# A two-layer trunk with 16 experts: one fixed tile per expert with its products in a new order, and the extra tiles in a loop of their own

## The chip, the core and the metric

The kernel runs on one core of one Trainium2 chip. The metric is the device time of one launch in microseconds (us). The engines are TensorE (PE in the profile, its weight loads PEld), VectorE (DVE), ScalarE (ACT), GpSimd (POOL) and SyncE (SP, which here only issues loads).

## The reference

Two layers (DEPTH = 2) work on 640 tokens of 1024 channels: 512 latent tokens and 128 context tokens. Each layer has an attention branch and a convolution branch, which are merged and projected, and then a mixture of experts. The change touches only the last:

```python
scores = softmax(t @ w_router)                  # 16 experts
# the best of 4 groups, then the best two experts in it; wsel: their scores, made to sum to 1
combine = sum(one_hot(eidx, 16) * wsel[..., None], axis=1)
hg = einsum('td,edf->tef', t, w_gate)           # 1024 -> 256
hu = einsum('td,edf->tef', t, w_up)
h = silu(hg) * hu * combine[..., None]
y = einsum('tef,efd->td', h, w_down)            # 256 -> 1024
```

All data are float32. Each token goes to 2 of 16 experts, so there are 1280 (token, expert) pairs in a layer, 80 an expert on average.

## The kernel before

Float32 products are made from two halves of each operand: a high half, which ScalarE writes as the engine's rounded format (hi, for experts `hi_expert`, L883), and a low half, raw minus high (lo, on POOL L1849 or VectorE L1222). A product takes three matmuls: high by high, high by low, low by high (`MM3`). Weights come in units of 1 MB through four raw buffers of 8 KB per partition: a load of unit n waits until unit n - 4 has its low half (`raw_free`). All engines have their programs written out by hand, and semaphores join them; the order in each engine's program is the order of its work.

An expert has three units. Before the change units 0 and 1 are the two halves of the 1024 input rows, with gate and up side by side (four pieces of 512 KB, in runs of 1 KB), unit 2 is down (runs of 4 KB).

**The routing** (VectorE L1564 to L1702) turns the router's logits into slots. TensorE's product with a triangle of ones gives each pair's place among its expert's pairs, a second product the counts (L688, L689; `place`). The pairs are sorted into tiles of 128 rows: an expert has ceil(count/128) tiles, at least one, and the tiles of all experts stand one behind the other. POOL writes ten columns of rows (token, target row, weight) into the table `tab_d` in memory (L1908), reads it back as `tab` (L1780), makes the low half of down of expert 0 (L1849), and starts to gather.

**The experts.** Every engine walks over the experts and, inside, over a loop with bounds that are read from `start_i` at run time (`value_load`). For a tile TensorE does, in this order: gate/up (24 matmuls, L718), the transposes of h (L724), the transposes of the next tile's gathered rows (8, L702), down (12 matmuls, L734). ScalarE does Silu (`sg`, L1168), the high halves of h (L1170) and of the gathered rows (L1134), drains down's result from PSUM to `ye` (L1141), and at an expert's start makes the high halves of the next expert's three units. VectorE does `hx` (L1731), the low halves of h (`ht_lo`, L1734) and of the gathered rows (`xt_lo`, L1713), and the low halves of the next expert's units. POOL gathers rows of `u2_d` by the table (L1931) and sends rows of `ye` to `y_d` (L1951). A table row that belongs to no pair gathers token 0; its send is skipped by the bounds check.

Of the next stage the experts' end releases this: ScalarE waits for the last send and reloads all results (`y_in`, L1178), VectorE adds them to `ha_in` (loaded by ScalarE's queue at the last expert, L1163).

The unit of work that waits and durations are given for below is a tile of 128 rows. `passed_X` semaphores only carry a wait over a branch.

Of the kernel before, what the change touches and what calls it, by code (L numbers as in the profile page):

```python
# [26 lines left out]
P = 128  # L27
D = 1024
DEPTH = 2
KC = D // P  # L30
# [14 lines left out]
MAXT = (2 * NTOK) // P + NE + 1  # L45
# [16 lines left out]
N_UNITS = U_MOE + 3 * NE  # L62

# [93 lines left out]
def _build(nc, io, out, ledger, ctx):  # L157
# [80 lines left out]
    xe = at("xe", [P, D], F32, R_Q)  # L238
    xt_hi = at("xt_hi", [P, KC, P], F32R, R_Q + 4 * KB)
    xt_lo = at("xt_lo", [P, KC, P], F32R, R_Q + 8 * KB)  # L240
    sg = at("sg", [P, DE], F32, R_Q + 12 * KB)
    hx = at("hx", [P, DE], F32, R_Q + 13 * KB)
    ht_hi = at("ht_hi", [P, 2, P], F32R, R_Q + 14 * KB)
    ht_lo = at("ht_lo", [P, 2, P], F32R, R_Q + 15 * KB)
    ye = at("ye", [P, D], F32, R_W)
    tab = at("tab", [P, MAXT, 4], U32, R_W + 4 * KB)
# [138 lines left out]
    def _(eng):  # L385
# [39 lines left out]
        for name in ("y_full", "gu_full"):  # L425
            eng.sem_inc(sems(name), 1)
        ledger.section = "layer"
        with eng.Fori(0, DEPTH) as l:
# [259 lines left out]
            mm(ps[:, b, 0:NT * NE], tri[:, :], cnt[:, :, :].rearrange("p t e -> p (t e)"), start=True, stop=True)  # L688
            ins = mm(ps[:, b, 256:256 + NT * NE], ones[:, :], cnt[:, :, :].rearrange("p t e -> p (t e)"), start=True, stop=True)  # L689
            ins.then_inc(*T.filled(("place",)))  # L690

            for b in range(8):
                eng.wait_ge(*T.at("drained", last[b]))
            eng.wait_ge(*T.at("starts"))
            eng.sem_inc(sems("passed_T"), 1)
            g0 = eng.value_load(start_i[0:1, NE + 1:NE + 2], min_val=1, max_val=DEPTH * MAXT)
            n0 = eng.value_load(start_i[0:1, NE + 2:NE + 3], min_val=0, max_val=DEPTH * MAXT)

            def xe_transposes(g):
# [5 lines left out]
            xe_transposes(g0)
            for e in range(NE):
                eng.wait_ge(*T.at("w_lo", U_MOE + 3 * e + 1))
                eng.sem_inc(sems("passed_T"), 1)
                i = (e + 1) % 2
                lo = eng.value_load(start_i[0:1, e:e + 1], min_val=0, max_val=MAXT - 2)  # L710
                hi = eng.value_load(start_i[0:1, e + 1:e + 2], min_val=0, max_val=MAXT - 2)
                with eng.Fori(lo, hi) as j:
                    g, n = g0 + j, n0 + j + 1

                    eng.wait_ge(sems("xt_split"), g)
                    for k in range(KC):
                        for w, x in MM3:
                            ins = mm(ps[:, 2, :], (xt_hi, xt_lo)[x][:, k, :], (gu_hi, gu_lo)[w][i][:, k, :],  # L718
                                     start=(k == 0 and w + x == 0), stop=(k == 7 and w == 1))
                    ins.then_inc(sems("gu_full"), 1)  # L720

                    eng.wait_ge(sems("h_ready"), n)
                    for c in range(2):
                        ins = nc.tensor.transpose(ps[:, 3, c * P:(c + 1) * P], hx[:, c * P:(c + 1) * P], ident[:, :])  # L724
# [50 lines left out]
    def _(eng):  # L775
# [7 lines left out]
        with eng.Fori(0, DEPTH) as l:  # L783
# [60 lines left out]
            for e in range(NE):  # L844
                if e > 0:
                    load_gate_up(e)
# [1183 lines left out]
```

## Time and profile before

| | |
|---|---|
| median of 3 runs | 2197.0 us (2195.05 to 2199.16) |
| profiled execution | 2203.22 us, its span 2201.6 us |
| PE, PEld busy | 1639.7 us (74%), 1383.9 us (63%) |
| DVE busy | 1380.1 us (63%) |
| ACT busy | 848.5 us (39%) |
| POOL busy | 526.1 us (24%) |
| granted TensorE clock, mean | 0.860 |
| moved by DMA | 307.20 MB, mean 140 GB/s |
| chain that ended last | PE 42%, DVE 20%, issue 18%, DMA 7%, POOL 5%, ACT 5% |

The profile is of one execution. Its times count from the span's start, and its own time is 1.6 us more than the span. Busy shares are means over stages with different limits, so the stages have to be read apart: the two stages of experts are from about 874 to 1083 us and from about 1946 to 2155 us. The chain is followed back from the last instruction to whatever released each step; "issue" in it is time in which an engine waited for nothing that the profile shows.

### The profile page before, as it was taken

The page shows a single profiled execution, that of the slowest core. Times are in us where ns is not written, and L with a number is a line of the kernel's source. Part 1 is how long each engine was busy: PE and PEld are TensorE (multiplying, and loading weights), DVE is VectorE, ACT ScalarE, POOL GpSimd, SP SyncE. Part 2 cuts the span into 40 slices and gives each one's busy share as a digit, 9 for nine tenths or more (in the row PEclk, how much of TensorE's full clock was granted, in tenths as well). Part 3 has the DMA queues.
Part 4 walks back from the last instruction along what each step waited for, and adds up shares of the span by engine and source line. Part 5 has one row for each costly group of instructions (what it writes and reads, how often), then busy time and mean ns, then how long its engine had stood idle before and what let it go on. Part 6 is the DMA issues. An engine that isn't in the chain of part 4 may idle for free.

```text
span 2201.6 us, 29454 instructions
## 1 busy us (share of the span) xinstructions
PE 1639.7 (74%) x8840; PEld 1383.9 (63%) x8840; DVE 1380.1 (63%) x2062; ACT 848.5 (39%) x1294; POOL 526.1 (24%) x338
## 2 busy tenths in 40 slices
PE   3798688888897951888448968887899886458880
PEld 1578455578897751667337965555899875446660
DVE  1457577889845353667562947778987256447754
ACT  3112455661123031667322225656311322147651
POOL 4222000014423213223223310000343232122231
PEclk6799789999999955999859978999899998579995
DMA  8121144312222531988821203441123162169975
GB/s 313 51 73 58 45 154 138 122 30 58 73 63 77 210 134 53 317 313 310 309 77 58 69 33 121 148 154 49 39 60 85 39 230 105 67 223 318 341 256 210
DMA packets 192595, 307.20 MB, mean 140 GB/s; under 512 B 10793, under 2 KB 146089, under 8 KB 185185
## 3 DMA queue, kind: packets, MB, share of 16 engines
q1 hardware_dynamic: 165696, 218.12, 30.3%
q0 software_dynamic: 16176, 46.23, 5.9%
q10 hardware_dynamic: 10560, 40.90, 4.9%
q8 instruction: 76, 1.25, 0.2%
q14 instruction: 87, 0.70, 0.1%
HBM read 275.58 MB, written 39.59 MB: 143 GB/s over the span
## 4 chain that ended last, share of the span: by engine, by line
PE 42%; DVE 20%; issue 18%; DMA 7%; POOL 5%; ACT 5%; DVEq 1%; ACTq 0%; POOLq 0%; SPq 0%
PE ps L472 10%; PE ps L458 5%; PE ps L650 5%; PE ps L718 4%; POOL w_lo L1852 4%; PE ps L536 4%; DMA raw<-in_w_down 3%; PE ps L734 3%; PE ps L404 2%; DVE probs L1393 2%; PE ps L516 2%; PE ps L680 1%; PE ps L545 1%; PE ps L518 1%; DVE gu_lo L1222 1%
## 5 line engine op out<-in xcount | busy, mean ns | idle before, releaser
L1852 POOL TENSOR_TENSOR w_lo<-raw,w_hi 128x2048 fp32r<-128x2048 f32 (+1 forms) x68 | 299.8, 4414 | 736.8 <-ACT w_hi L879 702.9
L472 PE MATMUL ps<-u_hi,w_hi 128*128 128x320 f32 x768 | 245.7, 320 | 41.5 <-POOL w_lo L1852 30.0
L879 ACT ACTIVATE w_hi<-raw 128x2048 fp32r<-128x2048 f32 (+1 forms) x68 | 109.2, 1610 | 357.2 <-PE ps L458 154.4
L472 PE MATMUL ps<-u_lo,w_hi 128*128 128x320 f32 x768 | 243.7, 317 | 0.0
L472 PE MATMUL ps<-u_hi,w_lo 128*128 128x320 f32 x768 | 243.3, 317 | 0.0
L1504 DVE SCALAR_TENSOR_TENSOR cv<-glu,convw,cv 128x670 f32<-128x670 f32 x240 | 234.6, 1056 | 0.0
L472 PEld LDWEIGHTS ps<-u_hi,w_hi 128*128 128x128 f32 x768 | 150.0, 195 | 45.2 <-issue 33.3
L1409 DVE TENSOR_TENSOR pt_lo<-ps,pt_hi 128x512 fp32r<-128x512 f32 x160 | 108.6, 690 | 67.3 <-ACT pt_hi L986 65.4
L472 PEld LDWEIGHTS ps<-u_lo,w_hi 128*128 128x128 f32 x768 | 150.0, 195 | 0.1
L472 PEld LDWEIGHTS ps<-u_hi,w_lo 128*128 128x128 f32 x768 | 150.0, 195 | 0.0
L986 ACT ACTIVATE pt_hi<-ps 128x512 fp32r<-128x512 f32 x160 | 93.4, 597 | 135.7 <-PE ps L536 134.7
L536 PE MATMUL ps<-ident,probs 128*128 128x128 f32 x640 | 109.3, 310 | 38.3 <-DVE probs L1393 32.4
L536 PEld LDWEIGHTS ps<-ident,probs 128*128 128x128 f32 x640 | 84.8, 159 | 69.5 <-DVE probs L1393 34.2
L1376 DVE TENSOR_REDUCE nmax<-ps 128x1 f32<-128x640 f32 x128 | 104.6, 817 | 33.4 <-PE ps L518 33.1
L458 PE MATMUL ps<-w_hi,u_hi 128*128 128x512 f32 x240 | 98.0, 408 | 30.7 <-DVE u_lo L1243 18.5
L963 ACT ACTIVATE probs<-ps,nmax 128x640 f32<-128x640 f32 x128 | 101.6, 794 | 42.1 <-DVE nmax L1376 38.6
L718 PE MATMUL ps<-gu_hi,xt_hi 128*128 128x512 f32 x272 | 108.2, 398 | 5.1 <-DVE xt_lo L1713 5.0
L1713 DVE TENSOR_TENSOR xt_lo<-ps,xt_hi 128x1024 fp32r<-128x1024 f32 x36 | 44.1, 1225 | 102.7 <-ACT xt_hi L1134 102.7
L718 PE MATMUL ps<-gu_hi,xt_lo 128*128 128x512 f32 x272 | 107.6, 396 | 0.0
L718 PE MATMUL ps<-gu_lo,xt_hi 128*128 128x512 f32 x272 | 107.3, 394 | 0.0
L516 PE MATMUL ps<-k_hi,q_st 128*128 128x320 f32 x256 | 90.4, 360 | 15.5 <-DVE q_st L1361 10.4
L458 PE MATMUL ps<-w_hi,u_lo 128*128 128x512 f32 x240 | 96.6, 403 | 0.0
(319 smaller groups left out, 4138.6 us busy)
## 6 DMA issues: line engine op xcount, KB each, us to landing
raw<-in_w_ada SPq DMA_DIRECT2D x52, 1024.0 KB, 4.9
raw<-in_w_in SPq DMA_DIRECT2D x48, 512.0 KB, 4.9
raw_x<-in_w_gate SPq DMA_DIRECT2D x32, 512.0 KB, 5.2
raw_x<-in_w_up SPq DMA_DIRECT2D x32, 512.0 KB, 6.4
raw<-in_w_down SPq DMA_DIRECT2D x16, 1024.0 KB, 8.5
raw<-in_w_gate SPq DMA_DIRECT2D x32, 512.0 KB, 4.4
raw<-in_w_up SPq DMA_DIRECT2D x32, 512.0 KB, 5.7
raw_x<-in_w_down SPq DMA_DIRECT2D x16, 1024.0 KB, 8.4
```

Of the source, the lines that this page charges most:

```text
L458: ins = mm(ps[:, bs[t], :], (u_hi, u_lo)[x][:, k, t * P:(t + 1) * P], (w_hi, w_lo)[w][:, s, c * 512:(c + 1) * 512], start=(k == 0 and w + ...
L472: ins = mm(ps[:, b, 0:HALF], (w_hi, w_lo)[w][:, s, cols(k):cols(k) + P], xs[x][:, k, half * HALF:(half + 1) * HALF], start=(k == 0 and w + ...
L516: mm(ps[:, b, 0:HALF], q_st[:, h % 2, t * P:(t + 1) * P], k_hi[:, g, i * HALF:(i + 1) * HALF], start=True, stop=False)
L536: ins = nc.tensor.transpose(ps[:, b, t * P:(t + 1) * P], probs[:, h % 2, t, kc * P:(kc + 1) * P], ident[:, :])
L650: ins = mm(ps[:, bs[t], :], (m_hi, m_lo)[x][:, k, t * P:(t + 1) * P], (w_hi, w_lo)[w][:, s, c * 512:(c + 1) * 512], start=(k == 0 and w + ...
L718: ins = mm(ps[:, 2, :], (xt_hi, xt_lo)[x][:, k, :], (gu_hi, gu_lo)[w][i][:, k, :], start=(k == 0 and w + x == 0), stop=(k == 7 and w == 1))
L879: act(w_hi[:, n % 2, 0:k], raw[:, n % 2, 0:k], ACT.Copy).then_inc(*A.up("a_hi", "w_hi", n))
L963: ins = act(probs[:, h % 2, t, :].rearrange("p (a b) -> p a b", a=2), ps[:, b0:b0 + 2, 0:HALF], ACT.Exp, bias=nmax[:, h % 2, t:t + 1], acc ...
L1376: v.tensor_reduce(nmax[:, h % 2, t:t + 1], ps[:, b0:b0 + 2, 0:HALF], axis=AX.XY, op=ALU.max, negate=True).then_inc(*V.up("v_max", "nmax", ...
L1409: v.tensor_tensor(pt_lo[:, k, :], ps[:, b, :], pt_hi[:, k, :].bitcast(F32), ALU.subtract).then_inc(*V.drained(("PT", h, kc)))
L1504: ins = v.scalar_tensor_tensor(out=cv[:, c, :], in0=src, scalar=convw[:, c, k:k + 1], in1=cv[:, c, :], op0=ALU.mult, op1=ALU.add)
L1852: g_.tensor_tensor(w_lo[:, n % 2, 0:k], raw[:, n % 2, 0:k], w_hi[:, n % 2, 0:k].bitcast(F32), ALU.subtract).then_inc(*G.up("g_lo", "w_lo", n))
```

## The change

1. **One fixed tile per expert.** The first 128 pairs of expert e are tile e; what an expert has beyond that goes to extra tiles 16, 17, ... (at most `OVT` = 9). The loop over 16 experts is written out with no run-time bounds and no counts read.
2. **New order on TensorE.** Gate/up of e, transposes of gathered rows of e+1, down of e-1, transposes of h of e. Gathered rows and results have two buffers each.
3. **Weights.** A unit is now gate, up or down whole, with input row p*8+c (down: p*2+c) on partition p, so that each partition's 8 KB are one run. The transposes take every eighth (second) column in return. The units' order is `GATE_UP_DOWN`: gate and up of e+2, then down of e+1. VectorE makes all three low halves in the loop; it also drains `ye` (ScalarE did). The first five units (gate, up and down of expert 0, gate and up of expert 1) get their low halves on POOL, all of them ahead of the writing of the table.
4. **Routing.** The sums over earlier token tiles are made by TensorE (20 products of 16 columns instead of 2 of 80), so VectorE's adds go; the extra tiles need a few new operations.
5. **Extra tiles.** After the 16 experts every engine runs a loop over n_over tiles (at least one, even if no expert has more than 128 pairs), which reads its expert's number, loads its three weights again, and does the tile's steps one after the other. `ha_in` is loaded behind it, and the send of expert 15's results stands behind the extra tile's in POOL's program.
6. Rows of no pair are skipped in gathers too; `xe` is zeroed once a layer for that.

The core of the diff:

```diff
-            mm(ps[:, b, 0:NT * NE], tri[:, :], cnt[:, :, :].rearrange("p t e -> p (t e)"), start=True, stop=True)
-            ins = mm(ps[:, b, 256:256 + NT * NE], ones[:, :], cnt[:, :, :].rearrange("p t e -> p (t e)"), start=True, stop=True)
+            for t in range(NT):
+                for i in range(t):
+                    mm(ps[:, b, t * NE:(t + 1) * NE], ones[:, :], cnt[:, i, :], start=(i == 0), stop=False)
+                mm(ps[:, b, t * NE:(t + 1) * NE], tri[:, :], cnt[:, t, :], start=(t == 0), stop=True)
+            for t in range(NT):
+                ins = mm(ps[:, b, 256:256 + NE], ones[:, :], cnt[:, t, :], start=(t == 0), stop=(t == NT - 1))
...
+            def xe_transposes(e):
+                eng.wait_ge(*T.at("xe_landed", e))
+                for k in range(KC):
+                    ins = nc.tensor.transpose(ps[:, k // 4, (k % 4) * P:(k % 4 + 1) * P], xe[:, e % 2, k:D:KC], ident[:, :])
+                ins.then_inc(*T.up("xt_full", "xt_full", e))
...
+            for e in range(NE):
+                eng.wait_ge(*T.at("xt_split", e))
+                eng.wait_ge(*T.at("w_lo", UNIT_OF[e, 0]))
+                eng.wait_ge(*T.at("w_lo", UNIT_OF[e, 1]))
+                gate_up((e + 1) % 2).then_inc(*T.up("gu_full", "gu_full", e))
+                if e + 1 < NE:
+                    xe_transposes(e + 1)
+                if e:
+                    down_of(e - 1)
+                eng.wait_ge(*T.at("h_ready", e))
+                h_transposes().then_inc(*T.up("ht_full", "ht_full", e))
+            down_of(NE - 1)
...
+            for e, k in GATE_UP_DOWN:
+                n = UNIT_OF[e, k]
+                load(n, (r(n, (KC, KC, 2)[k]), io[("w_gate", "w_up", "w_down")[k]][l, e, :, :].rearrange("(p c) n -> p c n", p=P)))
...
+            with eng.Fori(0, n_over) as j:
...
+                eng.wait_ge(sems("ov_dn_lo"), o)
+                over(0, 2)
+                eng.wait_ge(sems("ov_gu_lo"), 2 * o)
+                over(1, 3)
+                eng.wait_ge(sems("ov_gu_lo"), 2 * o + 1)
+                over(2, 2)
...
+            hi_expert(UNIT_OF[0, 2])
             eng.wait_ge(*A.at("u2_out"))
+            hi_expert(UNIT_OF[1, 0])
+            hi_expert(UNIT_OF[1, 1])
...
+            for e in range(NE):
+                eng.wait_ge(*V.at("gu_full", e))
+                eng.wait_ge(*V.at("sg_ready", e))
+                v.scalar_tensor_tensor(out=hx[:, :], in0=ps[:, 2, DE:2 * DE], scalar=tab[:, e, 2:3].bitcast(F32), in1=sg[:, :],
+                                       op0=ALU.mult, op1=ALU.mult).then_inc(*V.up("h_ready", "h_ready", e))
+                if e + 1 < NE:
+                    xt_lo_of(e + 1)
+                if e:
+                    y_of(e - 1)
+                eng.wait_ge(*V.at("ht_hi", e))
+                split_ht().then_inc(*V.up("ht_split", "ht_split", e))
+                if e + 2 < NE:
+                    lo(UNIT_OF[e + 2, 0])
+                    lo(UNIT_OF[e + 2, 1])
+                if e + 1 < NE:
+                    lo(UNIT_OF[e + 1, 2])
+            y_of(NE - 1)
...
-            for n in range(U_MOE, U_MOE + 2):
+            for n in range(U_MOE, U_MOE + 5):
                 lo(n)
...
-            lo(U_MOE + 2)
...
+            g_.memset(xe[:, :, :], 0.0).then_inc(*G.up("g_c", "xe_zero"))
...
+            for e in range(3):
+                gather_of(e)
             for e in range(NE):
+                if e + 3 < NE:
+                    gather_of(e + 3)
+                if e:
+                    scatter_of(e - 1)
...
+            with eng.Fori(0, n_over) as j:
...
+                gather(0, gidx[:, :]).then_inc(sems("ov_landed"), 16)
+                wait_apart("ov_hi", 3 * o)
+                g_.tensor_tensor(expert_part(1, 2, 0), over_raw(2, 2), expert_part(1, 2, 1).bitcast(F32), ALU.subtract).then_inc(sems("ov_dn_lo"), 1)
+                wait_apart("ov_ydrained", o)
+                scatter(0, sidx[:, :]).then_inc(sems("ov_sent"), 16)
+            scatter_of(NE - 1)
```

How it moves instructions, in three places. First POOL, from its last units ahead of the table to the first gathers. `gu_lo` and `dn_lo` are low halves of gate/up and down units; before:

```order
L1849 TENSOR_TENSOR gu_lo_98<-raw_x_50,gu_hi_96 128x2048
L1839 REGISTER_ALU
L1849 TENSOR_TENSOR gu_lo_98<-raw_x_51,gu_hi_96 128x2048
L1902 ISA
L1908 DMA tab_d<-rows,slot_u 3456x4 x10
L1910 ISA
L1780 DMA tab<-tab_d 128x27x4
L1839 REGISTER_ALU
L1849 TENSOR_TENSOR dn_lo_102<-raw,dn_hi_100 128x2048
```

and now:

```order
L1940 TENSOR_TENSOR gu_lo_98<-raw_x_51,gu_hi_96 128x8x256
L1930 REGISTER_ALU
L1940 TENSOR_TENSOR dn_lo_102<-raw,dn_hi_100 128x2048
L1930 REGISTER_ALU
L1940 TENSOR_TENSOR gu_lo_97<-raw,gu_hi_95 128x8x256
L1930 REGISTER_ALU
L1940 TENSOR_TENSOR gu_lo_97<-raw_x_50,gu_hi_95 128x8x256
L1994 ISA
L2000 DMA tab_d<-rows,slot_u 3200x4 x10
L2002 ISA
L1872 DMA tab<-tab_d 128x25x4
L2011 MEMSET xe 128x2048
```

Three subtractions stand ahead of the table's writing that were not there, and a memset stands behind its reload in place of the one that was.

Second TensorE, at the placement product (`cnt` are the 0/1 rows of pairs per expert); before:

```order
L688 MATMUL ps<-cnt,tri 128x80
L689 MATMUL ps<-cnt,ones 128x80
```

and now:

```order
L703 MATMUL ps<-cnt,tri 128x16
L702 MATMUL ps<-cnt,ones 128x16
L703 MATMUL ps<-cnt,tri 128x16
L702 MATMUL ps<-cnt,ones 128x16 x2
L703 MATMUL ps<-cnt,tri 128x16
L702 MATMUL ps<-cnt,ones 128x16 x3
L703 MATMUL ps<-cnt,tri 128x16
L702 MATMUL ps<-cnt,ones 128x16 x4
L703 MATMUL ps<-cnt,tri 128x16
L705 MATMUL ps<-cnt,ones 128x16 x5
```

Two products of 80 columns have become twenty of 16; each is a float32 product of two passes.

Third VectorE, one turn of the loop; before:

```order
L1731 SCALAR_TENSOR_TENSOR hx<-ps,wrow,sg 128x256
L1734 TENSOR_TENSOR ht_lo<-ps,ht_hi 128x256
L1712 ISA
L1713 TENSOR_TENSOR xt_lo<-ps,xt_hi 128x1024
L1724 REGISTER_ALU
L1724 COMPARE_AND_BRANCH
L1221 REGISTER_ALU
L1222 TENSOR_TENSOR dn_lo_101<-raw_x_51,dn_hi_99 128x2048
```

and now:

```order
L1793 SCALAR_TENSOR_TENSOR hx<-ps,tab,sg 128x256
L1771 TENSOR_TENSOR xt_lo<-ps,xt_hi 128x1024
L1786 COPY ye<-ps 128x1024
L1775 TENSOR_TENSOR ht_lo<-ps,ht_hi 128x256
L1284 REGISTER_ALU
L1285 TENSOR_TENSOR gu_lo_97<-raw_x_50,gu_hi_95 128x8x256
```

The drain of the results (`ye`) has come to VectorE, and the low half of the next gathered rows stands ahead of that of h.

## Rows read from the trace of the kernel before

**Rows 1.** Windows: stage, then its middle; busy us (instructions) per engine; clock, DMA share, GB/s.

```profile
873.90:1083.10 209.20, 173.53 (x782) 137.43 (x782) 137.42 (x113) 132.14 (x116) 59.73 (x68) 0.95 0.87 304
...
900.00:1040.00 140.00, 118.81 (x539) 94.32 (x538) 96.26 (x80) 92.10 (x80) 40.16 (x47) 0.95 0.90 312
```

**Rows 2.** Timeline: start, us, engine, line, operation; layer 0's 17th Silu.

```profile
1070.37 0.38 ACT L1168 ACTIVATE sg<-ps 128x256 f32<-128x256 f32 x1 [3.76 <-PE ps L718]
```

**Rows 3.** Chain of waits: start, us, what; first tile, two turns, layer 1's end.

```profile
873.86 7.97 PE ps L718 x24
...
1001.04 8.81 DMA raw<-in_w_down
...
1010.16 1.54 issue
...
1019.77 5.48 PE ps L718 x24
...
1027.86 3.02 PE ps L734 x12
...
2152.19 2.56 DMA y_d<-ye,sidx
2154.77 4.86 DMA y_in<-y_d
```

**Rows 4.** Groups of VectorE and ScalarE (count, busy, mean ns, idle); one timeline row.

```profile
L1713 DVE TENSOR_TENSOR xt_lo<-ps,xt_hi 128x1024 fp32r<-128x1024 f32 x36 | 44.1, 1225 | 102.7 <-ACT xt_hi L1134 102.7
L1731 DVE SCALAR_TENSOR_TENSOR hx<-ps,wrow,sg 128x256 f32<-128x256 f32 x34 | 16.4, 484 | 19.8 <-ACT sg L1168 19.7
L1734 DVE TENSOR_TENSOR ht_lo<-ps,ht_hi 128x256 fp32r<-128x256 f32 x34 | 14.4, 425 | 32.8 <-ACT ht_hi L1170 32.8
L1141 ACT ACTIVATE ye<-ps 128x1024 f32<-128x1024 f32 x36 | 36.3, 1009 | 19.4 <-DMA y_d<-ye,sidx 14.1 <-PE ps L734 5.3
996.53 4.49 DVE L1222 TENSOR_TENSOR gu_lo<-raw,gu_hi 128x2048 fp32r<-128x2048 f32 x2
```

**Rows 5.** Timeline of the routing and the table, layer 0.

```profile
823.78 1.89 ACT L883 ACTIVATE dn_hi<-raw 128x2048 fp32r<-128x2048 f32 x1
...
831.38 0.24 DVE L1629 TENSOR_TENSOR cnt<-msk 128x80 f32<-128x80 f32 x1
...
840.77 0.15 DVE L1701 SCALAR_TENSOR_TENSOR tbase<-start 128x1 f32<-128x1 f32 x1
841.99 1.09 POOL L1908 DMA_INDIRECT tab_d<-rows,slot_u  x1 [43.83 <-issue]
...
856.38 1.68 POOL L1780 DMA_DIRECT2D tab<-tab_d  x1 [1.75 <-DMA tab_d<-rows,slot_u]
...
864.80 1.11 POOL L1931 DMA_INDIRECT xe<-u_d,gidx  x1 [0.92 <-POOL gidx L1929]
```

**Rows 6.** DMA queues' sum for 5 to 21 us.

```profile
DMA packets 1190, 6.68 MB, mean 417 GB/s; under 512 B 96, under 2 KB 112, under 8 KB 640
```

**Rows 7.** VectorE beside POOL's subtractions (timeline).

```profile
787.33 10.83 POOL L1849 TENSOR_TENSOR gu_lo<-raw_x,gu_hi 128x2048 fp32r<-128x2048 f32 x2 [30.36 <-ACT gu_hi L883]
788.27 5.54 DVE L1559 SCALAR_TENSOR_TENSOR u<-h_a,rstd,a_row 128x1024 f32<-128x1024 f32 x1
...
1258.14 4.55 DVE L1274 TENSOR_TENSOR rot<-kr,rk 128x64 f32<-128x64 f32 x1
...
858.07 4.51 POOL L1849 TENSOR_TENSOR dn_lo<-raw,dn_hi 128x2048 fp32r<-128x2048 f32 x1
```

**Rows 8.** Timeline of TensorE: router products, a gather's eight transposes; their loads.

```profile
819.65 3.36 PE L680 MATMUL ps<-wr,u_t 128*128 128x16 f32 x15
...
1026.57 1.04 PE L702 MATMUL ps<-ident,xe 128*128 128x128 f32 x8
...
869.38 1.97 PE L702 MATMUL ps<-ident,xe 128*128 128x128 f32 x8 [36.56 <-DMA xe<-u_d,gidx]
...
L702 PEld LDWEIGHTS ps<-ident,xe x288: 139/140/230, 869.4 to 2146.5; 128*128 128x128 f32 x144
```

More of the change, by code:

```diff
@@ L44 @@
 CTX0 = NLAT + 2 * PAD
-MAXT = (2 * NTOK) // P + NE + 1
+OVT = (2 * NTOK) // (P + 1)
+MAXT = NE + OVT
 SKIP = 1 << 20
@@ L62 @@
 N_UNITS = U_MOE + 3 * NE
+GATE_UP_DOWN = [(0, 0), (0, 1), (0, 2), (1, 0), (1, 1)]
+for e in range(NE - 1):
+    GATE_UP_DOWN += [(e + 2, 0), (e + 2, 1)] if e + 2 < NE else []
+    GATE_UP_DOWN += [(e + 1, 2)]
+UNIT_OF = {ek: U_MOE + i for i, ek in enumerate(GATE_UP_DOWN)}
 MODW = 4 * 512
@@ L693, in _, with gate_up @@
                 eng.wait_ge(*T.at("drained", last[b]))
+            def xe_transposes(e):
[3 more added lines that the diff above has]
+                ins.then_inc(*T.up("xt_full", "xt_full", e))
+            def gate_up(i):
+                for k in range(KC):
+                    for w, x in MM3:
+                        ins = mm(ps[:, 2, :], (xt_hi, xt_lo)[x][:, k, :], (gu_hi, gu_lo)[w][i][:, k, :],
+                                 start=(k == 0 and w + x == 0), stop=(k == 7 and w == 1))
+                return ins
@@ new lines, in h_transposes, with down @@
+            def h_transposes():
+                for c in range(2):
+                    ins = nc.tensor.transpose(ps[:, 3, c * P:(c + 1) * P], hx[:, c:DE:2], ident[:, :])
+                return ins
+            def down(i):
+                for half in range(2):
+                    for c in range(2):
+                        for w, x in MM3:
+                            ins = mm(ps[:, 4 + half, :], (ht_hi, ht_lo)[x][:, c, :], (dn_hi, dn_lo)[w][i][:, c, half * 512:(half + 1) * 512],
+                                     start=(c == 0 and w + x == 0), stop=(c == 1 and w == 1))
+                return ins
@@ L705, in _ @@
[L705 to L724, printed above, removed]
-                    ins.then_inc(sems("ht_full"), 1)
-                    xe_transposes(g + 1)
-                    eng.wait_ge(sems("y_drained"), g)
-                    eng.wait_ge(sems("ht_split"), n)
-                    eng.wait_ge(*T.at("w_lo", U_MOE + 3 * e + 2))
-                    for half in range(2):
-                        for c in range(2):
-                            for w, x in MM3:
-                                ins = mm(ps[:, 4 + half, :], (ht_hi, ht_lo)[x][:, c, :], (dn_hi, dn_lo)[w][i][:, c, half * 512:(half + 1) * 512],
-                                         start=(c == 0 and w + x == 0), stop=(c == 1 and w == 1))
-                    ins.then_inc(sems("y_full"), 1)
@@ new lines, in _, with split_xt @@
+            eng.wait_ge(*V.at("v", V.steps))
+            v.tensor_scalar(start[:, 0:OVT], start[:, 0:OVT], float(NE - 1), None, ALU.min).then_inc(*V.step())
+            v.tensor_tensor(tbase[:, :], tbase[:, :], start[:, OVT:OVT + 1], ALU.add).then_inc(*V.step())
+            eng.wait_ge(*V.at("v", V.steps))
+            v.tensor_copy(start_i[:, :], start[:, :]).then_inc(*V.up("v_start", "starts"))
+            def split_xt():
+                return v.tensor_tensor(xt_lo[:, :, :].rearrange("p (a c) n -> p a (c n)", a=2), ps[:, 0:2, :],
+                                       xt_hi[:, :, :].rearrange("p (a c) n -> p a (c n)", a=2).bitcast(F32), ALU.subtract)
```

395 lines of the change are left out of this document (217 added, 178 removed).

## The prediction

> **What bounds the kernel now.** I read the stages first. Layer 0's experts run from the first gate/up product at 873.86 us to the issue of the results' reload at 1083.1; layer 1's reload starts at 2154.77 [rows 3]. The window row of that first stage shows TensorE busy 173.5 of 209.2 us at a granted clock of 0.95, VectorE 137.4, DMA 0.87 at 304 GB/s [rows 1]: nothing is full, so the stage is paced by waits. There are 34 tiles (hx x34 [rows 4]): 17 in a layer, 16 experts and one extra. The first Silu of layer 0 follows the end of its gate/up at 881.83 [rows 3], the 17th starts at 1070.37 [rows 2]: 11.8 us a tile.
>
> The chain of waits shows two sorts of turn. In the undisturbed one, gate/up starts at 1019.77, down (3.02) at 1027.86, and behind it the next gate/up [rows 3]: 11.1 us, of which 2.6 are a wait of TensorE between the end of gate/up (5.48) and down, while Silu, hx, its transposes and their halves are made. In the other one the chain goes through a weight load of 8.81 us and 1.54 us in which ScalarE reads loop bounds [rows 3]. The mean over the 16 steps, 11.8, is 0.7 above the good turn.
>
> **The routing ahead of it.** The chain of small VectorE operations ends its mask at 831.62 and the slots at 840.92; the table load is issued at 856.38, the first gather at 864.80 [rows 5], gate/up starts at 873.86. All of it is exposed.
>
> **The change, part by part.** I follow one layer; both have the same tiles.
>
> *The turn.* TensorE now does gate/up(e), gather transposes(e+1), down(e-1), transposes of h(e), so down covers the wait. Its work is 5.48 + 1.0 + 3.02 + 0.44, about 9.8 us with hand-overs. VectorE gets the drain of y as well. Three low halves cost 2.2 + 4.49 = 6.7 us (two take 4.49 back to back), xt_lo 1.23, hx 0.48, ht_lo 0.42 [rows 4]. The y drain is not there on VectorE; between the 1.0 us that ScalarE needs for it (ye [rows 4]) and 1.23 of xt_lo, which reads as many PSUM columns on VectorE, I take 1.2, nearer to the row of the same engine. Sum 10.03; I take 10.05 per expert, VectorE-bound, with TensorE 0.2 behind. Loads: an expert is 3.146 MB; gather and scatter move only real rows (80 a tile on average, both ways 0.65 MB), 3.80 MB in 10.05 us, or 378 GB/s. The old stage moved 312 GB/s in its middle at 0.90 busy [rows 1], so 347 when busy; the first loads of w_ada, in rows of 8 KB, ran at 417 GB/s [rows 6]. Gate and up now come in 8 KB rows too. I take 405, so the loads fit. The loads hide behind VectorE, and gathers are issued two turns ahead; if the rate were under 378, the load of a gate half would be late next.
>
> *Length of the fixed loop.* From the first gate/up to hx(0): 8.5 us (7.97 at the low clock [rows 3], Silu, hand-over). First turn 11.1, since xt_lo and the three halves come after an hx that was not late. 13 turns of 10.05 are 130.7. After hx(14): xt_lo(15) 1.8, gate/up(15) 5.5, down(14) 3.1, h transposes, its halves and y(14) 1.9, down(15) 3.1, drain 1.3, less 1.0 for what overlaps: 15.7. Together 166.
>
> *The extra tile.* It is serial. Count from the drain of y(15). Its gate and up are loaded before. POOL sends y(14), reads the count (the 1.54 row), copies two indices and gathers; by the old gather-to-transpose time of 4.6 us, rows land at about +3.4. Eight transposes at the low clock 1.97 [rows 8], xt_hi, of the size of ye's drain, 1.0 (with a hand-over +6.5), high half of up, which stands behind it on ScalarE, 1.9 as the one at 823.78 [rows 5] (+8.4), its low half 2.3 (+10.8), gate/up at the low clock 7.97 (+18.8), Silu to ht_lo 2.5 (+21.3), down 3.0 (+24.3), drain 1.2 (+25.5), POOL 0.9 to the send, and y(15), queued behind it, 1.3 later (+27.7), flight 2.56 (unloaded [rows 3]) or some more: +31. Down's weights: load issued at +4, 8.81 at worst, halves 1.9 + 4.5 [rows 7]: +19, under +21.3, covered. So the stage lasts 166 + 31 = 197 against 209.2: **-12.2 us**.
>
> *Placement products.* Two products of 80 columns (4 passes) become 20 of 16 columns, 40 passes, each with its own weights. The nearest row has 15 passes of exactly 128x16 in 3.36 us behind 818.8, 0.214 each with all 80 [rows 8]: 8.6 us, with VectorE idle behind them. The chain after them shrinks: by count of its dependent steps, 16 or so at 0.2 to 0.28, it is 4.9 us. Mask to slots is 0.15 + 8.6 + 4.9 = 13.6 against 9.3: **+4.3**.
>
> *Five low halves on POOL before the routing's table.* Before, POOL was idle for 43.8 us up to the first table send at 841.99 [rows 5]. Now it subtracts down(0) as soon as its high half is there (825.67 [rows 5]) and gate(1), up(1) behind it. What such a subtraction does to VectorE stands in [rows 7]: while POOL ran two of them (787.33, 10.83 us), a VectorE operation on 1024 columns (of the size for which xt_lo takes 1.23) took 5.54, and one of 64 columns took 4.55. Each waited for the whole POOL instruction, and VectorE got about one operation in between. 825.7 lies among the routing's chain, six us before the mask. Three subtractions of 4.51 [rows 7] hold it up by 13.5 us less the single operations between: **+13.3**. Bounds: 0, if the small operations slip by, and 16.3 with POOL's contended 5.4 each. I take the alternation that the rows show.
>
> *Start of the loop.* POOL's down(0) subtraction behind the table load (4.5) goes, and a memset of xe comes behind the table's landing: it reads nothing and lies between 0 and that subtraction's 4.51, and I take 1.9; index copies go. The gather followed the table issue by 8.4; I get 8.0: **-0.4**. The rest (no memset of ye at the start, fewer bound reads, h_a reload after the extra tile: it needs 13 us under load and is used 9 us later than y's reload; alone it takes about 8) I cost at nothing; its cover is y's own reload of 4.86 [rows 3] and, if gone, it costs up to 3 us a layer.
>
> *Sum.* Per layer -12.2 + 4.3 + 13.3 - 0.4 = +5.0, twice +10. The profiled execution took 2203.2 (span 2201.6), 6.2 above the median of 2197.0; scaled to it, **2207 us**. Its own range, from turns of 9.85 to 10.3 (-6, +7), overflow +-2 a layer, front +-2: 2196 to 2218.
>
> **Two rules that speak against it.** The first loads ran at 417 GB/s for 16 us [rows 6]. The Trainium skill's "DMA: Bandwidth & Descriptors", Specifications, puts the HBM limit per core at about 358 GB/s; by that rule the turn would be 3.80 MB / 358 = 10.6 us and the total, as an estimate, 2222. The trace does not agree, at least where one stream reads long rows. The eight transposes of a gather now read every eighth word. No row has such a read; the present ones take 1.04 us for eight [rows 8]. "Advanced Engine Details and Errata", Memory Cachelines, says of SBUF that a different 16-byte line per access brings a penalty, without a size.
>
> **Rivals.**
> A, *POOL does not hold the routing up* (the small operations slip between, or POOL comes late): the sum loses 13.3 twice, 2180 us, faster. It turns the sign from about 8 us of hold per layer downward. Against it: every two-operand VectorE operation from SBUF that met a POOL subtraction in [rows 7] waited it out. For it: none of those was as short as these.
> B, *the loads stay the bound*: at the old 347 GB/s a turn is 3.80/0.347 = 10.95, +0.9 x 28 = +25, 2232. For it: the DMA share was near full already; against it: 417 with long packets.
> C, *strided transposes*: if each of their weight loads doubles (0.14 to 0.28 us [rows 8]), eight add 1.1 us and more, say 1.3, TensorE's turn is 11.1 and the loop +1.05 x 28, with the extra tiles some 2240.
> D, *the change does not shorten the turn at all* (a stall like the 8.81 us load keeps 11.1): +1.05 x 28, also about 2236; I count it under B.
>
> **Chances.** Forecast case 0.60, A 0.17, B and D 0.13, C 0.10. A measurement of this kernel tells about 0.2% (4.4 us) from no change: faster below 2192.6, slower above 2201.4. A gives 0.16 and the forecast's lower edge 0.02: faster 0.18. Of the forecast case 0.13 lies within the band, with A's upper edge 0.14 in all. Slower 0.68. The range takes in A at its price and reaches up to most of B: 2178 to 2232, leaving out A's low side, C, and B's high side.
>
> **What would show it.** In the new profile: VectorE operations of 4 us and more between lg's exponential and the mask, three POOL subtractions side by side with them; 40 short passes behind the mask, 8 to 9 us; hx to hx 10.0 to 10.1 us with VectorE idle under 0.3 us a turn; TensorE clock at 1 throughout the loop; y(15) drained 166 us after the first gate/up, and 31 us more to the reload. Wrong if the turn is over 10.5 with VectorE waiting for weights' high halves (B), or with TensorE busy throughout (C), or if the mask comes within 8 us of down(0)'s high half (A).

## The result, and the profile after

The changed kernel takes 2220.7 us (median of 6 runs, 2209.3 to 2224.3) against 2196.7 us of the kernel before on the same chip: a ratio of 1.0108, with an interval from 1.0081 to 1.0135. It is slower by 24 us. The forecast was 2207, in a range from 2178 to 2232. The profiled execution has a span of 2217.3 us, 15.7 more than the one before. A second set of runs gave 1.0111 (1.0068 to 1.0154) and a span of 2220.1.

The stages stand side by side here; each number is the time (us) between the two points named in the first column, each of them the start or the end of a row.

| stretch | before, layer 0 / 1 | after, layer 0 / 1 | difference | forecast |
|---|---|---|---|---|
| exponential of lg to end of mask (cnt) | 8.02 / 8.01 | 19.11 / 19.13 | +11.1 | +13.3 |
| mask to end of slots (last tbase) | 9.30 / 9.31 | 14.78 / 14.78 | +5.5 | +4.3 |
| slots to first gate/up | 32.94 / 33.01 | 31.73 / 32.74 | -0.7 | -0.4 |
| first gate/up to issue of the results' reload | 209.26 / 209.07 | 202.70 / 201.28 | -7.2 | -12.2 |
| sum of a layer | | | +8.7 | +5.0 |

Twice 8.7 is 17.4. Layer 0's reload is issued 8.4 us later than before and layer 1's 15.0; attention and convolution between them, which the change does not touch, came out 1.9 us shorter. The medians differ by 24.0, 6.6 more than the sum. The two profiled executions differ by only 15.6, because that of before (2203.2) was 6.6 above the median of 2196.7 and that of after (2218.8) was 1.9 below its own.

**The routing.** VectorE's timeline of the changed kernel, beside POOL's, layer 0 (start, us, engine, line, operation):

```profile
825.37 0.17 DVE L1658 TENSOR_TENSOR pair<-sel 128x8 f32<-128x8 f32 x1
825.45 4.51 DVE L1659 TENSOR_TENSOR pair<-sel 128x4 f32<-128x4 f32 x1
829.88 0.16 DVE L1657 TENSOR_TENSOR pair<-sel 128x12 f32<-128x12 f32 x1
829.96 4.47 DVE L1658 TENSOR_TENSOR pair<-sel 128x8 f32<-128x8 f32 x1
834.35 0.15 DVE L1659 TENSOR_TENSOR pair<-sel 128x4 f32<-128x4 f32 x1
...
834.99 0.44 DVE L1667 MAX8 top<-g 128x8 f32<-128x8 f32 x5 [0.15 <-DVE g L1663]
...
836.40 2.49 DVE L1675 CAST ef<-idx 128x5 f32<-128x5 uint32 x1
...
842.10 0.24 DVE L1702 TENSOR_TENSOR cnt<-msk 128x80 f32<-128x80 f32 x1
```

```profile
825.38 4.55 POOL L1940 TENSOR_TENSOR dn_lo<-raw,dn_hi 128x2048 fp32r<-128x2048 f32 x1 [27.59 <-ACT dn_hi L948]
829.89 4.51 POOL L1940 TENSOR_TENSOR gu_lo<-raw,gu_hi 128x2048 fp32r<-128x2048 f32 x1
834.36 4.50 POOL L1940 TENSOR_TENSOR gu_lo<-raw_x,gu_hi 128x2048 fp32r<-128x2048 f32 x1
```

An addition of 8 columns, 0.17 us alone, takes 4.47: it ends with the POOL instruction beside it, as forecast from [rows 7]. One operation gets through between two of POOL's, as 829.88 does. The third subtraction met other work: a reduction, MAX8 and the searches, which take one tensor from SBUF, ran on undisturbed for 2 us. Only the cast at 836.40 was caught, though it has one input too; it ended at 838.89. That is why three subtractions cost 11.1 and not 13.3. Layer 1 repeats it (4.50, 4.47 and 2.49 us).

TensorE's placement products (timeline; the first and last group of 20 products in 40 passes) and VectorE behind them:

```profile
842.40 0.61 PE L703 MATMUL ps<-cnt,tri 128*128 128x16 f32 x2 [19.75 <-DVE cnt L1702]
...
848.82 2.29 PE L705 MATMUL ps<-cnt,ones 128*128 128x16 f32 x10
851.24 0.17 DVE L1720 COPY sca<-ps 128x16 f32<-128x16 f32 x1 [7.29 <-PE ps L705]
...
856.97 0.15 DVE L1766 TENSOR_TENSOR tbase<-tbase,start 128x1 f32<-128x1 f32 x1
```

They take 8.7 us at a granted clock of 0.50 (8.6 forecast); the chain behind them takes 5.9 where I had counted 4.9. The two products of 80 columns took 1.15 us in the kernel before (831.67 to 832.82).

**The loop.** Windows of the changed kernel: the two stages and the middle of layer 0's loop, columns as in [rows 1]:

```profile
888.90:1091.50 202.60, 170.76 (x774) 138.43 (x774) 151.69 (x113) 114.34 (x96) 62.29 (x34) 0.95 0.79 296
1968.50:2169.80 201.30, 172.32 (x774) 139.41 (x774) 151.49 (x113) 113.94 (x96) 64.90 (x34) 0.93 0.76 288
905.00:1040.00 135.00, 125.00 (x590) 102.29 (x589) 123.81 (x91) 93.55 (x77) 50.58 (x25) 0.99 0.97 366
```

In the middle the DMA engines are 0.97 busy at 366 GB/s (0.90 and 312 in [rows 1]), and VectorE idles 11.2 of 135 us. From the first hx (896.44) to the 15th (1044.39) are 14 turns in 147.95 us, in layer 1 145.68: 10.5 a turn (10.6 in layer 0, 10.4 in layer 1), where 10.05 was forecast. What VectorE waited for between 905 and 1040 (view of waits: total us, times, longest):

```profile
DVE dn_lo L1285 <- ACT dn_hi L948: 7.1, 9, 1.5
DVE gu_lo L1285 <- ACT gu_hi L948: 2.8, 4, 1.4
DVE ye L1786 <- PE ps L733: 0.9, 3, 0.5
```

Those high halves wait for their loads in turn. ScalarE waited 32.3 us for loads of weights in this window; the two longest entries are

```profile
ACT gu_hi L948 <- DMA raw_x<-in_w_up: 9.6, 6, 2.8
ACT dn_hi L948 <- DMA raw_x<-in_w_down: 8.7, 6, 1.9
```

**The extra tile** (timeline, layer 0: y(15) drained, the gather, gate/up, and the reload):

```profile
1059.66 1.23 DVE L1786 COPY ye<-ps 128x1024 f32<-128x1024 f32 x1 [3.29 <-PE ps L733]
1059.93 1.06 POOL L2020 DMA_INDIRECT xe<-u_d,gidx  x1 [0.90 <-POOL sidx L2057]
...
1070.52 0.80 PE L720 MATMUL ps<-gu_hi,xt_hi 128*128 128x512 f32 x1 [5.24 <-DVE gu_lo L1817]
...
1091.55 1.73 ACTq L1242 DMA_DIRECT2D y_in<-y_d  x2
```

From 1060.89 to the reload 30.7 us, in layer 1 30.4 (31 forecast).

### The profile page after: what moved, and what is told of

It is laid out like the page before. It is cut to its first block, busy times and chain, and to the rows that moved or that the text cites. A ratio compares the mean times of both kernels' runs of the same rounds, so it can differ in the third digit from the quotient of the medians.

```text
span 2217.3 us, 27630 instructions
## 1 busy us (share of the span) xinstructions
PE 1648.4 (74%) x8896; PEld 1400.1 (63%) x8896; DVE 1428.9 (64%) x2051; ACT 820.3 (37%) x1260; POOL 558.6 (25%) x273
## 4 chain that ended last, share of the span: by engine, by line
PE 41%; DVE 22%; issue 18%; DMA 8%; POOL 5%; ACT 5%; DVEq 1%; ACTq 0%; POOLq 0%; SPq 0%
PE ps L484 10%; PE ps L470 5%; PE ps L662 5%; POOL w_lo L1943 4%; PE ps L548 4%; PE ps L720 4%; DMA raw_x<-in_w_down 3%; PE ps L416 2%; DVE probs L1456 2%; PE ps L528 2%; DVE gu_lo L1285 2%; DMA raw<-in_w_down 2%; PE ps L557 2%; PE ps L692 1%; PE ps L530 1%
## 5 line engine op out<-in xcount | busy, mean ns | idle before, releaser
L484 PE MATMUL ps<-u_hi,w_hi 128*128 128x320 f32 x768 | 245.1, 319 | 40.6 <-POOL w_lo L1943 30.7
L720 PE MATMUL ps<-gu_hi,xt_hi 128*128 128x512 f32 x272 | 114.9, 422 | 32.0 <-DVE xt_lo L1771 21.3
L1439 DVE TENSOR_REDUCE nmax<-ps 128x1 f32<-128x640 f32 x128 | 104.5, 816 | 32.3 <-PE ps L530 31.8
L2025 POOL DMA_INDIRECT y_d<-ye,tab x32 | 70.7, 2211 | 119.9 <-DVE ye L1786 109.8
L1351 DVE TENSOR_TENSOR sq<-q_tok 128x512 f32<-128x512 f32 x20 | 29.6, 1478 | 105.2 <-ACT q_tok L980 104.7
```

The lines of the kernel that those rows point to most:

```text
L484: ins = mm(ps[:, b, 0:HALF], (w_hi, w_lo)[w][:, s, cols(k):cols(k) + P], xs[x][:, k, half * HALF:(half + 1) * HALF], start=(k == 0 and w + ...
L1439: v.tensor_reduce(nmax[:, h % 2, t:t + 1], ps[:, b0:b0 + 2, 0:HALF], axis=AX.XY, op=ALU.max, negate=True).then_inc(*V.up("v_max", "nmax", ...
```

## The experiments

All times are medians beside the kernel before on the same chip and in the same set. Line numbers in rows of an experiment are those of its own kernel, a few off from the changed one's.

**1. The changed kernel again.** No edit.

> The changed kernel itself, once more beside the kernel before, as the base for the others. The two profiled executions differ by 15.7 us of span, the medians of the first runs by 24.0. If the part that the profiles do not show is only the spread between executions, the difference comes out between 15 and 24 us again, and the loop of layer 0 (first hx to 15th) lies within 2 us of 147.9.

2221.8 us against 2198.3 (+23.5). 14 turns took 145.1 and 147.4 us, so layer 0's loop is 2.9 us shorter than in the first profile, a little beyond the 2 us named. The stretches from the exponential to the table load were the same to 0.02 us. In these two executions the routing repeats exactly, the loop does not.

**2. The three subtractions on VectorE.** The first loop is POOL's, the second VectorE's.

```diff
-            for n in range(U_MOE, U_MOE + 5):
+            for n in range(U_MOE, U_MOE + 2):
                 lo(n)
...
             v.tensor_copy(start_i[:, :], start[:, :])...
+            for n in range(U_MOE + 2, U_MOE + 5):
+                lo(n)
```

> The three subtractions down(0), gate(1) and up(1) leave POOL and stand on VectorE behind the cast of start_i, where VectorE idled 30 us until the first gathered rows. Theory (POOL's subtractions hold VectorE's two-operand operations for their whole length): the mask comes 10.7 us earlier in each layer, no VectorE operation between the exponential and the mask is over 0.6 us, and the total falls by 20 to 22 us. Rival 1 (the chain was late for another reason, such as ScalarE's high halves at the same time): the mask moves by less than 3 us and the total by less than 6. Rival 2 (the loads behind these three units start 27 us later and the loop starves at its start): the mask moves by 10.7, but the first three turns of the loop take 2 to 5 us more and the total falls by 10 to 17 only.

2198.9 us: 22.9 less than the changed kernel of the same set, and 1.0008 (0.9989 to 1.0028) of the kernel before. The mask comes 8.14 us after the exponential in both layers, 11.0 sooner:

```profile
828.88 0.24 DVE L1702 TENSOR_TENSOR cnt<-msk 128x80 f32<-128x80 f32 x1
```

The theory holds for the mask, and rival 1 is out. So is rival 2: the loop's first three turns took 10.8, 11.2 and 10.4 us (10.5, 9.9 and 12.5 in layer 1), as long as the changed kernel's 10.5, 9.9 and 12.7 (10.8, 11.2 and 9.6). A price of another kind showed. While VectorE subtracts, POOL's instructions that send the table's rows take longer:

```profile
844.04 2.31 DVE L1285 TENSOR_TENSOR dn_lo<-raw,dn_hi 128x2048 fp32r<-128x2048 f32 x1
845.41 1.85 POOL L2002 DMA_INDIRECT tab_d<-rows,slot_u  x1 [0.30 <-issue]
846.28 2.28 DVE L1285 TENSOR_TENSOR gu_lo<-raw,gu_hi 128x2048 fp32r<-128x2048 f32 x1
...
851.91 0.98 POOL L2002 DMA_INDIRECT tab_d<-rows,slot_u  x1 [0.30 <-issue]
```

Three of them take 1.84 to 1.90 us instead of 0.98, and slots to table load is 2.6 us longer.

So the stretches that the edit touches gain 2 x (11.0 - 2.6) = 16.7 us, and not all of the 22.9. Of the other 6, 4.4 lie ahead of the first routing and between the layers, where the two kernels do the same work, and 1.7 in the stages of experts. The start of layer 0's exponential varies from 820.98 to 823.82 us among the profiles of kernels that are the same up to there, so this rest is not shown to come from the edit.

**3. Two placement products of 80 columns.**

```diff
-            for t in range(NT):
-                for i in range(t):
-                    mm(ps[:, b, t * NE:(t + 1) * NE], ones[:, :], cnt[:, i, :], ...)
-                mm(ps[:, b, t * NE:(t + 1) * NE], tri[:, :], cnt[:, t, :], ...)
...
+            mm(ps[:, b, 0:NT * NE], tri[:, :], cnt[:, :, :]..., start=True, stop=True)
+            ins = mm(ps[:, b, 256:256 + NT * NE], ones[:, :], cnt[:, :, :]..., ...)
```

VectorE sums over the groups of tokens again, as in the kernel before (not shown).

> The 20 products of 16 columns go back to two of 80, with the sums over the groups of tokens made on VectorE as before; all else as changed. Theory (the short products cost what their passes take): mask to the end of the slots falls from 14.8 us to between 9 and 10.5, the total by 9 to 12 us. Rival (the sums on VectorE, ten dependent steps of 0.2 to 0.25 us, eat most of it): mask to slots stays above 12 us and the total falls by under 5.

2212.5 us, 9.3 less; mask to slots 9.85 us in both layers. The theory holds: the ten steps on VectorE are cheaper than the passes that they save, by 4.9 us a layer.

**4. Short rows, neighbouring columns.**

```diff
-                    ... xe[:, e % 2, k:D:KC], ident[:, :])
+                    ... xe[:, e % 2, k * P:(k + 1) * P], ident[:, :])
...
-                load(n, ... .rearrange("(p c) n -> p c n", p=P)))
+                load(n, ... .rearrange("(c p) n -> p c n", p=P)))
```

The same in the extra tiles and for hx.

> The weights' rows of gate and up are 1 KB again (and 4 KB for down), input row c*128+p on partition p, and the transposes read 128 neighbouring columns; all else as changed. Theory A (the loop's 10.5 us turn is held by the loads, and long rows make the rate): busy DMA rate falls from 379 towards the 347 GB/s of the kernel before, the turn goes to 10.9 or 11.0, the total rises by 11 to 15 us. Theory B (the rate has a ceiling of its own that does not hang on the rows' length): the turn stays within 0.15 us of 10.5 and the total within 4 us. Theory C (the strided transposes are what stretches the turn): the turn falls to 10.1 and the total by 10 us; their eight passes would fall well below 1.04 us.

2231.6 us, 9.8 more (somewhat under theory A's 11 to 15); 14 turns took 153.3 and 151.4 us, 10.9 a turn, as theory A says. The window of its loop:

```profile
905.00:1040.00 135.00, 123.74 (x583) 99.17 (x583) 118.97 (x85) 88.16 (x73) 50.67 (x24) 0.98 1.01 349
```

With short rows the DMA engines are full at 349 GB/s. Long rows are therefore worth 0.4 us of the 1.3 by which the turn fell (11.8 to 10.5). The other 0.9 is there with short rows too and comes with the rest of the change, the order and the fixed tiles, which no run takes apart. As for the transposes, the weight loads and passes of the changed kernel, then of this one (ns, min/median/max):

```profile
L714 PEld LDWEIGHTS ps<-ident,xe x256: 185/188/226, 884.3 to 2121.4; 128*128 128x128 f32 x128
L714 PE MATMUL ps<-ident,xe x256: 272/273/482, 884.3 to 2121.5; 128*128 128x128 f32 x128
```

```profile
L714 PEld LDWEIGHTS ps<-ident,xe x256: 138/140/230, 885.0 to 2135.9; 128*128 128x128 f32 x128
L714 PE MATMUL ps<-ident,xe x256: 270/272/476, 885.0 to 2136.0; 128*128 128x128 f32 x128
```

Every eighth word costs 48 ns in a weight load and nothing in a pass, behind which the load is hidden. The Trainium skill ("Advanced Engine Details and Errata", Memory Cachelines) names a penalty when each access touches another line of SBUF, without a size; the rows give 48 ns here. The turn did not fall when it went, so theory C is out.

**5. Half the bytes.**

```diff
-                load(n, (r(n, ...), io[...][l, e, :, :].rearrange("(p c) n -> p c n", p=P)))
+                part = c if e < 2 else c // 2
+                load(n, (r(n, c)[:, 0:part, :], io[...]...[:, 0:part, :]))
```

> From expert 2 on each unit's load brings only the first half of each partition's run (4 KB of 8), so that half of these experts' weights are what lay there before; the order, the waits and the work of all engines stay. Only layer 0's loop is read, since layer 1 then routes other data. It had 145.1, 148.0, 146.8 and 150.7 us from the first hx to the 15th in four profiles with the changed loop (10.36 to 10.77 a turn). Theory (the loads add the part above VectorE's 10.05): 14 turns take 140 to 143 us, the DMA share falls from 0.97 to about 0.6, and no VectorE subtraction waits for a high half. Rival (the extra comes from engines waiting on each other, whatever the loads): 145 us or more.

From expert 2 on each load leaves out the second half of every partition's run, so half of these experts' weights are what lay there before. 14 turns took 138.5 us, below the 140 to 143 expected: 9.9 a turn, and from the third turn on 9.6 and 9.8 by turns, 9.7 on the average. No subtraction of VectorE waited for a high half. The total was 2201.1 us, which says little, since layer 1 routes other data. Window of the loop:

```profile
905.00:1035.00 130.00, 128.61 (x621) 106.81 (x620) 127.50 (x93) 95.28 (x80) 49.17 (x25) 1.00 0.70 227
```

The engines' own turn is thus 9.7, not 10.05. TensorE (128.6 of 130 us) and VectorE (127.5) are both nearly full, so the run does not say which of them holds it. All above that, 0.8 us a turn, comes with the loads.

**6. The drain of y on ScalarE.** Added to ScalarE's loop, taken from VectorE's.

```diff
+                if e:
+                    eng.wait_ge(*A.at("y_full", e - 1))
...
+                    act(ye[:, (e - 1) % 2, :]..., ps[:, 4:6, :], ACT.Copy)...
...
-                if e:
-                    y_of(e - 1)
```

> In the fixed loop the drain of y goes back to ScalarE, between the high half of gate(e+2) and that of h; VectorE has 1.2 us less in a turn (8.85), TensorE 9.8. Theory (the loads are what holds the turn, near 370 GB/s): the 14 turns stay at 145 to 149 us and the total within 5 us of 2221. Rival (VectorE is what holds it, and the loads only now and then): 138 to 141 us, the total down by 12 to 18. Rival 2 (ScalarE's later high halves of h hold down back): above 150.

2218.2 us, 1.0089 (1.0066 to 1.0113) of the kernel before: with the changed kernel's 1.0111 of the other set, 0.2% less, within what the two intervals leave open. 14 turns took 145.1 and 143.7, in layer 1 a little under the theory's 145. VectorE was busy 108.7 of 130 us, the DMA engines 0.98 at 372 GB/s. Taking 1.2 us a turn from VectorE gives back less than 0.2, so VectorE is not what holds the turn.

**7. All first low halves on VectorE.** The first loop is POOL's; the second stands on VectorE behind the normalised tokens, the third ahead of its wait for the table.

```diff
-            for n in range(U_MOE, U_MOE + 5):
-                lo(n)
...
             k_fixed = V.steps
+            for n in range(U_MOE, U_MOE + 3):
+                lo(n)
...
+            eng.wait_ge(*V.at("tab_row", 1, NT - 1))
...
+            for n in range(U_MOE + 3, U_MOE + 5):
+                lo(n)
```

ScalarE makes down(0)'s high half behind the router's third pair of drains.

> All five first low halves are made by VectorE: gate(0), up(0) and down(0) behind the normalised tokens, while TensorE works on the router, gate(1) and up(1) once the last table row has landed; ScalarE makes down(0)'s high half between the router's transposes. POOL subtracts nothing there. Theory (the whole POOL instruction holds VectorE, here too): TensorE's wait of 8.92 us for the second tile of normalised tokens goes, exponential to mask takes 8.1 us, slots to table load 14.5; the total falls by 2 x (11.0 + 8.9) = 40 us against the changed kernel, to about 2182. Rival (the high halves among the router's drains, or later loads, take it back): router to exponential gains less than 5 us, and the total comes to 2190 or more.

2186.9 us, 0.995 (0.9931 to 0.9969) of the kernel before. From the first transposes of the router to its first reader are 26.1 us (782.90 to 809.03), where the changed kernel has 34.6 (788.12 to 822.68): 8.4 us, which the kernel before pays as well (8.92 us of wait there too, behind its two subtractions of [rows 7]). It missed 2182 by 5 us. Two loads of 1 MB now start beside the load of the table (849.24 and 851.58, the table's at 847.29), and table load to gather took 10.7 and 11.9 us instead of 8.2; experiments 10 and 11 show that this is their doing. The 14 turns took 149.7 and 148.1.

**8. Which POOL instruction holds VectorE.** The kernel of experiment 7 with two clears and two copies on POOL.

```diff
+            eng.wait_ge(*G.at("w_hi", U_MOE))
+            for k in range(2):
+                g_.memset(to, 0.0)...
+            for k in range(2):
+                g_.tensor_copy(to, expert_raw(U_MOE))...
```

> The kernel of the run named five, in which POOL is idle while VectorE normalises the tokens; here POOL does, from gate(0)'s high half on, two clears of 128x2048 and then two copies of 128x2048 from one place of SBUF to another. In the changed kernel two subtractions stood there and two of VectorE's operations took 5.53 and 5.40 us. Theory 1 (any POOL instruction on SBUF holds VectorE's two-operand operations): operations of 1.8 us and more beside the clears, of a copy's length beside the copies. Theory 2 (only POOL instructions that read SBUF do): nothing over 1.4 us beside the clears, longer ones beside the copies. Theory 3 (only those that read two operands): no operation over 1.4 us at all.

Timeline of VectorE and POOL:

```profile
789.89 1.80 POOL L2006 MEMSET junk<- 128x2048 f32 x1 [0.15 <-POOL junk L2006]
...
790.11 1.22 DVE L1627 TENSOR_TENSOR u<-u,b_row 128x1024 f32<-128x1024 f32 x1
...
791.25 1.28 DVE L1624 SCALAR_TENSOR_TENSOR u<-h_a,rstd,a_row 128x1024 f32<-128x1024 f32 x1
...
791.87 2.41 POOL L2010 COPY junk<-raw_x 128x2048 f32<-128x2048 f32 x1 [0.18 <-POOL junk L2006]
792.56 2.79 DVE L1627 TENSOR_TENSOR u<-u,b_row 128x1024 f32<-128x1024 f32 x1
...
795.28 2.91 DVE L1624 SCALAR_TENSOR_TENSOR u<-h_a,rstd,a_row 128x1024 f32<-128x1024 f32 x1
```

Nothing is held beside the clears; beside the copies 1.22 becomes 2.79 and 1.28 becomes 2.91, to 1.1 us past the copy's end at the most. Layer 1 has the same durations. That is theory 2: POOL must read SBUF. A copy has one operand, so theory 3 is out too. The Trainium skill ("SBUF — State Buffer", Who interferes with whom) states this: a VectorE instruction with two SBUF inputs contends with a GpSimd instruction that reads SBUF, not with one that only writes it. The trace agrees, on both sides.

**9 to 11. The parts together.** Experiment 7 with experiment 3 and xe's clearing behind the issue of the table's load; then two variants with the clearing ahead of the table's sends and the drain on ScalarE. The two variants, 10 and 11, differ only in the place of the low halves of gate(1) and up(1): beside the table's sends (10) or, as in experiments 7 and 9, behind the landing of its last row. Their edits are not printed.

> The kernel of the run named five, with the two placement products of 80 columns, and with the clearing of xe moved from behind the table's landing to behind its load's issue (1.8 us and a hand-over each layer). If the parts add up: 2182 - 9 - 4 = about 2169, 1.3% under the kernel before. If the loop, held by loads that now start later before it, gives back 3 us a layer, 2175.

2174.8 us, 0.9885 (0.986 to 0.991) of the kernel before: 1.15% faster than that, and by the two ratios 2.2% faster than the changed one. The mask comes 8.05 us after the exponential, the slots 9.85 after it. The loop gave back what the expectation allowed: 151.7 and 147.7 us. On POOL the clearing is hidden, but the table's landing is late, as in experiment 7:

```profile
847.55 1.61 POOL L1885 DMA_DIRECT2D tab<-tab_d  x1 [1.74 <-DMA tab_d<-rows,slot_u]
849.14 1.83 POOL L2018 MEMSET xe<- 128x2048 f32 x1
856.52 1.09 POOL L2031 DMA_INDIRECT xe<-u_d,tab  x1 [5.55 <-DMA tab<-tab_d]
```

> The kernel of the run named best, with xe cleared before the table's rows are sent (POOL is idle there), gate(1) and up(1)'s low halves directly behind the cast of start_i instead of behind the table's landing, and y drained by ScalarE in the loop. In best the table took 9.0 us from issue to the first gather instead of 5.5 plus the clearing, beside two loads of 1 MB, and the loop took 151.7 and 147.7 us. Theory (the loads' late start costs both): table sends lose 1.8 us to VectorE's two subtractions, table load to gather falls to 6.5, the 14 turns to 146; with the drain's 2 us a layer, the total is 2160 to 2166. Rival (the loads only collide with something else, the sends): no better than 2172.

> As best2, but with gate(1) and up(1)'s low halves where best has them, behind the landing of the last table row. If the position of these two decides, it is 3 to 8 us slower than best2; if only the clearing and the drain do, the two are within 2 us.

2172.8 (0.9885, 0.9869 to 0.990) and 2171.0 (0.9885, 0.9865 to 0.9906). The first missed its 2160 to 2166 and is at its rival's 2172: table load to gather fell to 6.2 us and the sends took 1.7 longer, both about as expected, but the 14 turns stayed at 151.9 and 148.6 us (147.8 and 148.7 in the second). The first gather of experiment 10, then that of experiment 11:

```profile
854.36 1.08 POOL L2034 DMA_INDIRECT xe<-u_d,tab  x1 [4.56 <-DMA tab<-tab_d]
```

```profile
850.48 1.08 POOL L2036 DMA_INDIRECT xe<-u_d,tab  x1 [7.13 <-DMA tab<-tab_d]
```

The table's load landed 5.2 us after its issue in experiment 10 and 7.7 in experiment 11, where two loads of 1 MB are issued 1.9 and 4.3 us behind it. That single difference shows the collision. In the total it is offset by the sends, and the two are within 2 us, so the position of the two low halves does not decide. All three kernels stand at 0.9885 of the kernel before, so what the clearing and the drain are worth together is not told from noise.

## Why the prediction was right, and where it was off

The direction and its two causes were right. **POOL's low halves ahead of the table** cost 11.1 us a layer (13.3 forecast). Taking them away brings the mask 11.0 us sooner in each layer; the total fell by 22.9, of which 16.7 are seen in the edited stretches (experiment 2). What was mis-sized is the step "13.5 us less the single operations between": the third subtraction met operations that it does not hold. Rival A, that the small operations slip by, is out for those with two inputs and true for reductions, MAX8 and the searches. **The placement products** cost 5.5 instead of 4.3: the passes were right, the chain behind them, "16 or so" dependent steps, is 1.0 us longer than my count of it. Undoing them gave back 9.3 us in all.

**The stage of experts** gained 7.2, not 12.2. The extra tile was right within 0.6. What failed is the fixed loop, 166 us forecast and 172.0 and 170.9 measured, and in it two steps with opposite errors. VectorE's sum of 10.05 was too high: without the load of the other halves the turn is 9.7 (experiment 5). The terms given for TensorE add to 9.94, not to about 9.8, and are above 9.7 too. "I take 405, so the loads fit" was wrong: the loop moves 366 to 372 GB/s with the DMA engines at 0.97 or 0.98, so the turn is 10.5. The 405 leaned on 417 GB/s, which I had read as one stream in rows of 8 KB [rows 6]. It is not: the same view of the kernel before, from 5 to 21 us, shows two queues (packets, MB, share), of which q1 brings the weights and q0 is POOL's:

```profile
q1 hardware_dynamic: 630, 4.51, 67.4%
q0 software_dynamic: 560, 2.17, 33.7%
```

In the loop gathers and scatters run beside the loads. That these lower the rate there is not shown. The rule that I set against it (the Trainium skill, "DMA: Bandwidth & Descriptors", Specifications, about 358 GB/s, an estimate of 10.6 a turn and 2222 in all) came nearer than my rate, though the loop's mean is above its figure. In kind this is rival B: VectorE idled 0.9 us a turn, not under 0.3, and waited for weights' high halves, with a turn of 10.6 in layer 0. At B's price, 10.95, the experiment with short rows lies (10.9 a turn). So the changed kernel stands between my case and B. Its 2220.7 is above the 2196 to 2218 that I gave the forecast case alone; it is inside the whole range because that was widened towards B.

Rival C is out: the strided weight loads cost 48 ns more each and stay hidden. Rival D is out as well: the turn did fall, from 11.8 on the mean to 10.5.

The errors of the routing, -2.2, +1.2 and -0.3 a layer, and the stage's +5.0 leave 3.7 a layer over the forecast, or 7.4 in all; less the 1.9 between the layers, that is the 5.5 or so by which the profiled difference of 15.7 exceeds the forecast's 10. So the number is near partly because the errors of the routing offset one another. The further distance to the median is the spread between executions: the loop's 14 turns took 144 to 152 us in the kernels with full loads and long rows, with no cause that the runs separate. It stays open why experiments 7 and 9 to 11 have longer loops (147.7 to 151.9). Over the same part of the loop as the changed kernel's window their DMA share is 0.95 to 0.97 at 357 to 367 GB/s, so the loads fill the DMA engines there too, at a slightly lower rate. The late start of the loads is not shown to be it, since experiment 8, which makes its low halves at the same places as 7, had 144.2 and 145.3.

## What to carry to other kernels

Work that fills an idle engine is not free because the engine was idle: ask which other engine computes beside it, with what operands. Here 13.5 us of POOL cost VectorE's chain of 0.2 us operations 11 us, while VectorE itself had 30 idle us for the same work a little later, at a price of 2.6 us to POOL's sends. And when a loop's waits are removed, check the next resource at the mean rate that the loop's own mixture of transfers reaches, not at the best rate of another stretch.

## What the runs showed of the hardware

- A POOL instruction that reads SBUF (subtraction 4.5 us, copy 2.4) holds a VectorE operation with two inputs from SBUF until it is over: additions of 128x4 and 128x8, 0.17 us alone, took 4.51 and 4.47. Beside a clear (1.8 us) an operation of 1.22 us kept its 1.22. MAX8 (0.44 us for five), searches (0.16) and a reduction (0.28) went on beside the subtraction; a cast of 128x5 was held (2.49).
- It works the other way too: while VectorE subtracts 128x2048, POOL's issue of an indirect transfer takes 1.85 us instead of 0.98 (experiments 2 and 10).
- A table of 50 KB lands 5.2 us after its load's issue when no weights are loaded beside it, and after 7.6 to 8.0 us with two loads of 1 MB issued behind it (experiments 7, 9 and 11, layer 0).
- A transpose's weight load of 128x128 32-bit values at a distance of 8 words takes 188 ns instead of 140, its pass 272 either way.
- With gate and up in rows of 8 KB the changed loop moved 366 to 373 GB/s at a DMA share of 0.97 to 0.98; with rows of 1 KB it moved 349 to 358 at 1.01.
